# A hybrid encoder layer on one core: a token's score with itself by two 512-column products with ones

## The reference

```
qh = sigmoid(hq);  vh = silu(hi)
f  = lb + (1 - lb) * sigmoid(f_logit);   k = 1 - f;   g = log(f)
scores[t, s] = sum_k q[t, k] * exp(b[t, k] - b[s, k]) * k[s, k]      for s <= t
o = scores @ v + (q * exp(b)) @ state
...
o = rmsnorm(o_fwd + o_bwd, hg_out_norm) * silu(hg)
```

## Time and profile before

| | |
|---|---|
| median of 3 runs | 1032.99 us (1032.89 to 1034.73) |
| the profiled execution's own time | 1034.0 us |
| its span, first to last instruction | 1032.2 us |
| TensorE busy | 1018.5 us (99%) |
| DVE, ACT, POOL busy | 413.7, 361.4, 449.3 us |
| mean granted TensorE clock | 0.999 |

### The profile page before, as it was taken

One profiled execution on the slowest core, in us unless ns is written; L12 is line 12 of the kernel. 1 busy time (PEld: TensorE's weight loads), 2 busy tenths in 40 slices (PEclk: granted clock), 3 DMA queues, 4 the chain that ended last, 5 costly groups with the idle time before them and its releaser, 6 DMA issues.

```text
span 1032.2 us, 13344 instructions
## 1 busy us (share of the span) xinstructions
PE 1018.5 (99%) x5063; PEld 860.5 (83%) x5063; DVE 413.7 (40%) x568; ACT 361.4 (35%) x577; POOL 449.3 (44%) x299
## 2 busy tenths in 40 slices
PE   8999999999999999999999999999999999999997
PEld 7988888888888887888898988898888888888886
DVE  4443343443101073186647586543434434410103
ACT  6322222222223164447566564532222222222321
POOL 3444444444444444837344333334444444344440
PEclk9999999999999999999999999999999999999999
DMA  8333333332433234422210123222333333323312
GB/s 237 93 101 102 95 92 98 102 100 84 133 111 100 86 94 105 114 70 84 62 42 22 52 80 105 82 83 84 98 102 100 92 93 102 102 88 117 102 42 82
DMA packets 136476, 96.26 MB, mean 93 GB/s; under 512 B 11586, under 2 KB 120403, under 8 KB 136436
## 3 DMA queue, kind: packets, MB, share of 16 engines
q1 hardware_dynamic: 136256, 95.70, 31.1%
q10 hardware_dynamic: 180, 0.02, 0.0%
HBM read 93.27 MB, written 2.10 MB: 92 GB/s over the span
## 4 chain that ended last, share of the span: by engine, by line
PE 91%; DVE 5%; issue 1%; ACT 1%; DMA 1%; POOL 0%; DVEq 0%; SPq 0%; ACTq 0%
PE ps L911 18%; PE ps L913 18%; PE ps L912 18%; PE ps L919 9%; PE ps L920 9%; PE ps L918 9%; PE ps L1087 2%; PE ps L1200 1%; PE ps L936 1%; DVE W L1493 1%; PE ps L1187 1%; PE ps L1174 1%; DVE SD L1508 1%; DMA X<-x 1%; DVE YB L1370 1%
## 5 line engine op out<-in xcount | busy, mean ns | idle before, releaser
L442 POOL TENSOR_TENSOR WL<-raw,WH 128x1024 fp32r<-128x1024 f32 x132 | 317.1, 2404 | 421.4 <-ACT WH L521 421.4
L911 PE MATMUL ps<-XH,WH 128*128 128x512 f32 (+1 forms) x944 | 355.6, 377 | 0.1
L913 PE MATMUL ps<-XH,WL 128*128 128x512 f32 (+1 forms) x944 | 354.3, 375 | 0.0
L912 PE MATMUL ps<-XL,WH 128*128 128x512 f32 (+1 forms) x944 | 354.3, 375 | 0.0
L521 ACT ACTIVATE WH<-raw 128x1024 fp32r<-128x1024 f32 x162 | 171.0, 1056 | 318.6 <-PE ps L913 167.6
L913 PEld LDWEIGHTS ps<-XH,WL 128*128 128x128 f32 x944 | 178.0, 189 | 32.1
L911 PEld LDWEIGHTS ps<-XH,WH 128*128 128x128 f32 x944 | 178.2, 189 | 31.0 <-issue 0.5
L912 PEld LDWEIGHTS ps<-XL,WH 128*128 128x128 f32 x944 | 178.1, 189 | 30.5
L918 PE MATMUL ps<-WH,hh 128*128 128x512 f32 x352 | 137.1, 389 | 0.0
L920 PE MATMUL ps<-WL,hh 128*128 128x512 f32 x352 | 137.0, 389 | 0.0
L919 PE MATMUL ps<-WH,hl 128*128 128x512 f32 x352 | 136.9, 389 | 0.0
(11 more groups left out here) (177 smaller groups left out, 849.4 us busy)
## 6 DMA issues: line engine op xcount, KB each, us to landing
raw<-ffn_w_gate SPq DMA_DIRECT2D x44, 512.0 KB, 3.9
raw<-ffn_w_up SPq DMA_DIRECT2D x44, 512.0 KB, 3.9
raw<-ffn_w_down SPq DMA_DIRECT2D x44, 512.0 KB, 3.8
raw<-w_in SPq DMA_DIRECT2D x22, 512.0 KB, 4.0
raw<-w_out SPq DMA_DIRECT2D x8, 512.0 KB, 3.3
X<-x SPq DMA_DIRECT2D x4, 512.0 KB, 7.7
raw<-w_in SPq DMA_DIRECT2D x8, 256.0 KB, 3.6
out<-X SPq DMA_DIRECT2D x8, 256.0 KB, 2.0
```

Source lines behind the costliest of these rows:

```text
L442: pool.tensor_tensor(low, raw[:, s, :], high.bitcast(fp32), ALU.subtract).then_inc(lo_done, 1)
L911: nc.tensor.matmul(dst, WH[:, s, w], xh, start=first, stop=False)
L912: nc.tensor.matmul(dst, WH[:, s, w], xl, start=False, stop=False)
L913: return nc.tensor.matmul(dst, WL[:, s, w], xh, start=False, stop=last)
```

## The change

KS no longer holds the sum of the keys but its product with the queries, element by element; so the score of token t with itself is the sum of column t over the 128 partitions. TensorE makes that sum by products with a matrix of ones, over all 512 tokens at once: one with the high part DGH, one with the low part DGL. ACT makes DGH (diag_split), DVE makes DGL (diag_low), which lies on KS. The result has the sum in every row; diagonal(h) is as before. The masks are kept without their repeat over the chunks, at another place in SBUF, and the predicated copy repeats them by its access pattern.

```diff
-        m = np.zeros((P, 2, TT, P // (2 * h), h), np.float32)
+        m = np.zeros((P, 2, P // (2 * h), h), np.float32)
...
-                pool.tensor_tensor(KS[:, :], W[:, b, K_B, :], W[:, b, K_F, :], ALU.add).then_inc(base_ready, 1)
+                pool.tensor_tensor(KS[:, :], W[:, b, K_B, :], W[:, b, K_F, :], ALU.add).then_inc(key_summed, 1)
+                pool.wait_ge(key_summed, h + 1)
+                pool.tensor_tensor(KS[:, :], KS[:, :], Qh[:, b, :], ALU.mult).then_inc(base_ready, 1)
...
+            def diag_split(h):
+
+                act.wait_ge(base_ready, h + 1)
+                if h:
+                    act.wait_ge(scores_ready, 11 * (h - 1) + 1)
+                nc.scalar.activation(DGH[:, :], KS[:, :], ACT.Copy).then_inc(diag_high, 1)
...
+            diag_split(0)
             for k in range(BEATS):
                 h, g = divmod(k, 11)
...
                         out_gate_sigmoid(n)
                     else:
                         copy_unit(n)
+                if h < NH - 1 and g == 10:
+                    diag_split(h + 1)
...
-                    pe.wait_ge(base_ready, h + 1)
+                    pe.wait_ge(diag_ready, h + 1)
...
-                    for c in range(TT):
-                        mm = nc.tensor.matmul(to[:, chunk(c)], KS[:, chunk(c)], Qh[:, b, chunk(c)], start=True, stop=True)
+                    nc.tensor.matmul(to[:, :], ones_r[:, :], DGH[:, :], start=True, stop=False)
+                    mm = nc.tensor.matmul(to[:, :], ones_r[:, :], DGL[:, :], start=False, stop=True)
...
-                nc.vector.tensor_tensor(KS[:, :], W[:, b, K_B, :], W[:, b, K_F, :], ALU.add).then_inc(base_ready, 1)
+                nc.vector.tensor_tensor(KS[:, :], W[:, b, K_B, :], W[:, b, K_F, :], ALU.add).then_inc(key_summed, 1)
+                dve.wait_ge(key_summed, h + 1)
+                dve.wait_ge(proj_sig, 1)
+                nc.vector.tensor_tensor(KS[:, :], KS[:, :], Qh[:, b, :], ALU.mult).then_inc(base_ready, 1)
+
+            def diag_low(h):
+
+                dve.wait_ge(base_ready, h + 1)
+                dve.wait_ge(diag_high, h + 1)
+                nc.vector.tensor_tensor(DGL[:, :], KS[:, :], DGH[:, :].bitcast(fp32), ALU.subtract).then_inc(diag_ready, 1)
...
-                nc.vector.copy_predicated(SD[:, h % 2, :].rearrange("p (b s j) -> p s b j", s=2, j=half), masks[:, lv, :],
+                nc.vector.copy_predicated(SD[:, h % 2, :].rearrange("p (b s j) -> p s b j", s=2, j=half),
+                                          masks[:, lv, :, :].unsqueeze(2).broadcast_to([P, 2, TT, P // 2]),
                                           ps[4 + (11 * h + 1 + lv) % 2][:, :]).then_inc(scores_masked, 1)
...
+            nc.vector.memset(ones_r[:, :].bitcast(fp32), 1.0)
             wide_values()
             key_sum(0)
+            diag_low(0)
...
+                if h < NH - 1 and g == 10:
+                    diag_low(h + 1)
```

More of the change, by code:

```diff
@@ L105, in host_tables @@
                 hit = (s // (2 * h) == b) & ((s // h) % 2 != side)
-                m[:, side, :, b, :] = hit[:, None, None]
-        levels.append(m.reshape(P, TOK))
+                m[:, side, b, :] = hit[:, None]
+        levels.append(m.reshape(P, P))
     return {
@@ L138, in encoder_layer @@
         MS0, MS1, MST, ROOT_Y, R_Y, MSX, ROOT_X, R_X = range(8)
-        sb("row_pad", [P, 296])
+        masks = sb("masks", [P, 7, 2, P // 2], u8)
+        sb("row_pad", [P, 72])
         X = sb("X", [P, TT, D])
@@ L160, in encoder_layer @@
         hid = [place((f"hh{f}", [P, KF, TOK], f32r), (f"hl{f}", [P, KF, TOK], f32r)) for f in (1, 2)]
-        V, W, Fg, QS, KK, VA, GT, Qh, KS, SD, SX, KM, masks, rope, _, band = place(
+        V, W, Fg, QS, KK, VA, GT, Qh, KS, SD, SX, KM, DGH, ones_r, _, rope, _, band = place(
             ("V", [P, TT, TOK], fp32), ("W", [P, 2, 4, TOK], fp32), ("Fg", [P, 2, 2, TOK], fp32),
@@ L164, in encoder_layer @@
             ("GT", [P, 2, TOK], fp32), ("Qh", [P, 2, TOK], fp32), ("KS", [P, TOK], fp32),
-            ("SD", [P, 2, TOK], fp32), ("SX", [P, 3, TOK], fp32), ("KM", [P, 2, TOK], fp32), ("masks", [P, 7, TOK], u8),
+            ("SD", [P, 2, TOK], fp32), ("SX", [P, 3, TOK], fp32), ("KM", [P, 2, TOK], fp32), ("DGH", [P, TOK], f32r), ("ones_r", [P, P], f32r), ("mask_pad", [P, 2 * P], fp32),
             ("rope", [P, 2, TOK], fp32), ("rope_pad", [P, P], fp32), ("band", [P, 3 * P], fp32))
@@ L174, in encoder_layer @@
             ("ELb", [P, 2, SLOT], f32r))
+        _, DGL = place(("to_DGL", [P, 66 * K], fp32), ("DGL", [P, TOK], f32r))
         _, S = place(("to_S", [P, 85 * K + K // 2], fp32), ("S", [P, SRING, 3 * P], fp32))
@@ L210, in encoder_layer @@
         keys_grown, keys_mixed = sem("keys_grown"), sem("keys_mixed")
+        diag_ready, diag_high = sem("diag_ready"), sem("diag_high")
+        key_summed = sem("key_summed")
         base_ready, gated, tree_ready = sem("base_ready"), sem("gated"), sem("tree_ready")
```

## The result

The changed kernel takes 1047.85 us (median of 4 runs, 1046.24 to 1049.71) against 1032.94 us (4 runs, 1032.78 to 1034.73): a ratio of 1.0142, interval 1.0130 to 1.0155. It is 14.9 us slower. The forecast was 7.5 us slower, with 1044.5 us as the upper end. The direction and the place were right, the size was not.

What follows compares the result with a forecast made beforehand. TensorE, holding 91% of the span, was taken to bound the kernel. Losses at the four head starts, 3.1 + 2.0 + 1.6 + 0.8 = 7.5 us, carried in full, gave 1033.0 + 7.5 = 1040.5 us, range 1036.5 to 1044.5.

Steps and rivals of the forecast that it cites:

- What bounds the kernel, where the change acts, that the pauses carry to the end: TensorE bounds the kernel; the change acts at scores(h, 0) of four heads; their 7.5 us carry fully to the end.
- ACT's order as the cause of the pauses, and the copy's price: At four head starts, DGH's copy waits behind ACT's queued work, then takes 0.62 us (bounds 0.58 and 0.86).
- The first product behind a wait, 0.47 us instead of 0.23: At each head's start, TensorE's first 512-column product after waiting for DGL takes 0.47 us instead of 0.23.
- the clock: Across the four pauses, TensorE's clock stays at 1.00; its fall adds nothing to the 7.5 us sum.
- head 0's subtraction: At head 0's start, DVE's subtraction making DGL takes 0.89 us beside a busy POOL; dearest case 1.77 us.
- rival 4: Head 0's 3.1 us pause lowers TensorE's clock, costing 4.1 us more, up to 1044.6 us; chance 0.05.
- POOL's extra product at nothing: Heads 1 to 3: product delays POOL's decay tree by 1.3 us, covered by a full beat, so costs nothing.
- The masks, the memset, the saving on TensorE: Masks and memset cost nothing; ones-products at four head starts save TensorE 0.43 us once, 0.49 three times, 1.9 in all.
- rival 1: Pauses partly repaid: waits elsewhere in the mixer shrink by 1.5 to 4.8 us, giving 1035.7 to 1039.0 us; chance 0.15.
- rival 2: Masks' new pattern makes wide-run predicated copies cost 1.31 instead of 0.70 us: 1043.5, up to 1046 us; chance 0.07.
- rival 3: Subtractions in heads 0 and 1 at 1.77 us, copies at 0.86: 2.9 us more, 1043.4 us; chance 0.07.
- rival 5: Not slower: DGL ready before TensorE asks at head starts, only the 1.9 us gain stands, 1031.1 us; chance 0.03.

Runs made afterwards that it cites:

- experiment 1: Changed kernel with all four DGH copies moved ahead of TensorE's last product before the head: 1033.47 us, ratio 1.0000 to the kernel before.
- experiment 2: Changed kernel with only head 0's DGH copy moved early, in front of the loop over FIRST: 1041.05 us, ratio 1.0068 to the kernel before.
- experiment 3: Changed kernel with only the DGH copies of heads 1 to 3 moved ahead of the beat's exponential: 1040.24 us, ratio 1.0068 to the kernel before.
- experiment 5: Changed kernel with 16, 6, 6 and 4 idle products in front of TensorE's waits for DGL: 1044.08 us, ratio 1.0102 to the kernel before.
- experiment 6: Changed kernel with POOL starting the low part of unit 12's weights only after head 0's subtraction: 1045.25 us, ratio 1.0112 to the kernel before.
- experiment 10: Changed kernel with all DGH copies early and heads 1 to 3's elementwise product moved from POOL to DVE: 1031.36 us, ratio 0.9987 to the kernel before.
- experiment 9: Kernel before the change with only the masks' part of the change added: 1032.89 us against 1032.87, ratio 1.0000.
- experiment 7: Changed kernel with POOL's unit 12 after head 0's subtraction and 11, 6, 6, 4 idle products before TensorE's waits: 1041.25 us, ratio 1.0081 to before.

## Why the prediction fell short

*What bounds the kernel, where the change acts, that the pauses carry to the end:* right. Experiments 1 to 3 give back 14.4 of 14.9 us by moving four copies.

*ACT's order as the cause of the pauses, and the copy's price:* right. The copy took 0.61 to 0.62 us for 0.62, and in the profile after, heads 1 to 3 wait 2.35, 2.01 and 1.26 us, where the prediction had said 2.3, 1.8 and 1.1 (it said 3.3 for head 0).

*The first product behind a wait, 0.47 us instead of 0.23:* too much. The 0.47 is the length of a record, the 0.23 a step between starts. The step was 0.31 us behind the wait at 404.91 in the trace before, and 0.31 and 0.30 us in heads 1 and 3 after the change: 0.16 us too much a head.

*Two steps failed, the clock and head 0's subtraction.* Together they are 6.4 us; the clock is the larger.

*The clock, put at nothing in the sum:* wrong, by 3.8 us (experiment 5). With the clock held up the changed kernel takes 1044.08 us; with POOL's part cured and the clock left to fall it still takes 1045.25 (experiment 6). The prediction knew the mechanism: rival 4 had it with a chance of 0.05, for head 0 alone, since "the other pauses are shorter" and a wait of 1.52 us had left the clock at 1.00. Against head 0's own pause it named no reason, though its rows said that an idle time of about that length can do it. And the other pauses were no safer: the clock fell behind head 0 and behind head 2 in the profiled execution.

The page "TensorE: Matmul & The Clock Gate" of the Trainium skill, section "What's actually happening", has an idle TensorE fall to half clock. The runs agree on the two levels; behind a pause of 2.01 us they show the fall only when products were running again.

*Head 0's subtraction, 0.89 us in the sum, with 1.77 as its bound:* wrong, it took 2.80 us. The prediction's reason was "in this very stretch such an instruction took 0.89". That is a row in which DVE got in between POOL's pieces: it started at 434.95, inside a piece of POOL's that ended by 435.3, and POOL's next piece, from 435.25, took 1.19 us instead of 0.74. So the row shows a wait for one piece, and then POOL waiting for DVE. The subtraction after the change did not get in at the next three ends of pieces, and was held until POOL's whole series ended. The worth of this step is 2.6 us (experiment 6), with what the shorter pause does to the clock. Why one instruction got in and the other did not stays open.

The nearest row by kind was the same subtraction in the feed-forward stage, in the page's groups (line 1398 before, 1414 after):

```profile
L1414 DVE TENSOR_TENSOR hl<-SQ,hh 128x512 f32 x44 | 118.6, 2696 | 5.4
```

It takes 2.70 us beside one POOL instruction of 2.40: in the trace before, one such pair runs from 701.72 to 704.41 and from 701.48 to 703.88, and the subtraction ends 0.53 us behind POOL, as it does in head 0. Had the row been an end of the range, head 0 would have been priced up to 1.8 us dearer. Its number would have fitted by luck, for there DVE waits for one long instruction and here for a series of short ones.

The page "SBUF — State Buffer" of the Trainium skill, section "Who interferes with whom", has a DVE instruction with two SBUF inputs and a GpSimd instruction that reads SBUF contend for an exclusive lock. The trace agrees that one waits the other out. Worked out for one piece of POOL's, as the prediction did it, the rule gives 1.44 us, nearer than 0.89; but one piece, 0.74 us, was not the unit here, as the 2.80 us and POOL's end at 435.97 show.

*POOL's extra product at nothing:* wrong by 0.8 us, as the small waits show. The cover, a full beat for the first user of the tree, held for that user, but not at the head's end, where DVE is the one behind. Experiment 10 removes them.

*The masks, the memset, the saving on TensorE:* right (the masks by experiment 9; for the rest, experiment 10 comes within 0.4 us of the whole gain of 1.9).

The account, from 7.5: 0.8 for the waits that POOL's product makes, which gives 8.3 us as experiment 7 measured; 2.6 for the subtraction (experiment 6) and 3.8 for the clock (experiment 5) make 14.7 of the 14.9 us. The last two were cured one at a time and overlap in the clock; both cures together (experiment 7) gave back 6.6 us, close to their sum of 6.4.

Of the rivals, 1 (repaid in part) and 2 (masks) did not occur, 3 was too small at 1.77 us, 4 occurred, and behind head 2 as well as head 0, and 5 is what experiments 1 and 10 made of the kernel.

## What to carry to other kernels

When an operand is made by a chain over several engines, find for each link what stands in front of it in its engine's order, and move the link before touching its cost: here the places of four copies were worth 14.4 us and the new products 1.5 to 1.8. A pause of the busiest engine costs its length and, in some executions, nearly as much again in clock (3.45 and 2.6 us here); price it from the products behind it at both levels, and do not leave the clock out because the pause is short. When a DVE instruction with two SBUF inputs meets a busy POOL, let the rest of the series that POOL has queued set the dear end of the range (2.80 us here), and not the median of its kind (0.70).

## What the runs showed that was not expected

TensorE's clock fell behind pauses of 2.01 us (head 2 after the change) and 2.34 us (head 1 in experiment 2), and there it fell when products were running again, 0.2 and 1.1 us behind the first weight load. The length of the pause does not decide it alone: behind head 1's pause of 2.35 us it did not fall after the change, and did in experiment 6, 1.5 us behind the first weight load. It fell even at the end of head 3, behind waits of 1.29 and 0.55 us, in the profiled executions of experiments 1 and 3, and not in that of the kernel before, which has the same two waits. What decides it stays open.

With a pause of 3.45 us, four of six executions took 2.6 us more than the other two, with mean clocks of 0.996 against 0.998 and 1.000.

DVE's subtraction waited out a series of POOL's, the rest of one piece and three more (2.1 us beyond its own 0.70), and not one piece alone; it did so in three profiled executions (2.80, 2.88 and 2.80 us). With POOL's series ended, it took 0.69 us.
